# First attention of a hybrid decoder step: token rows on partitions, the norm in a later stage, the combination one step later, the big jobs in the first 24 prompt steps

## The reference, cut to what matters

```
aq, ak = rmsnorm(...), rmsnorm(...)              # 4 heads, two 64-wide maps each
s = einsum('bqhcd,bkhcd->bhcqk', q, k) * scale   # c = 0, 1: the two maps
s = where(dist >= 0, s + bias, -inf)             # causal, ALiBi
p = softmax(s, axis=-1)
a = p[:, :, 0] - lam * p[:, :, 1]
oa = einsum('bhqk,bkhd->bqhd', a, v)
oa = rmsnorm(oa, g_oa) * (1.0 - lam_init)        # over the 128 values of a head
ua = (oa.reshape(B, T, 512) * silu(az)) @ w_branch[0]
```

## Time and profile before

| | us |
|---|---|
| three timed runs, median (lowest to highest) | 1586.78 (1585.46 to 1587.12) |
| the profiled execution, its own time | 1587.19 |
| its span, from the first to the last instruction | 1585.0 |
| PE busy, share of the span | 1507.2, 95% |
| DVE, ACT, POOL busy | 585.4, 397.1, 82.4 |
| mean granted PE clock, share of full | 0.975 |

### The profile page before, as it was taken

How to read it: one execution, slowest core, us unless ns; L and a number is a source line. 1 busy time by engine, 2 the same in 40 slices (tenths; PEclk the granted TensorE clock), 3 DMA queues, 4 the chain that set the end, 5 groups by cost and what they waited for, 6 DMA issues and landing times.

```text
span 1585.0 us, 17452 instructions
## 1 busy us (share of the span) xinstructions
PE 1507.2 (95%) x6810; PEld 1027.9 (65%) x6810; DVE 585.4 (37%) x1321; ACT 397.1 (25%) x874; POOL 82.4 (5%) x109
## 2 busy tenths in 40 slices
PE   6899998999977999999999999999999999999998
PEld 3477665566645544465666665645888778999586
DVE  2444444566565313014545323243333223221321
ACT  2322222444443113102221202123232122121200
POOL 0000001000000000000000000000111101111000
PEclk9899999999997899999999998999999999999999
DMA  9211001010002240000101023100012233210232
GB/s 322 85 60 48 27 30 57 1 54 1 1 0 89 81 149 27 0 20 20 41 21 40 24 60 100 40 1 0 21 49 92 85 109 127 54 47 21 59 100 67
DMA packets 77521, 88.39 MB, mean 56 GB/s; under 512 B 7634, under 2 KB 55394, under 8 KB 77442
## 3 DMA queue, kind: packets, MB, share of 16 engines
q1 hardware_dynamic: 74082, 76.15, 15.7%
q0 software_dynamic: 3360, 11.14, 1.9%
HBM read 76.14 MB, written 11.14 MB: 55 GB/s over the span
## 4 chain that ended last, share of the span: by engine, by line
PE 91%; DVE 3%; ACT 2%; issue 1%; SPq 1%; DMA 1%; POOL 0%; POOLq 0%; DVEq 0%; ACTq 0%
PE heavy L848 32%; PE heavy L794 12%; PE heavy L763 9%; PE heavy L764 9%; PE heavy L765 9%; PE attended L961 2%; PE attended L913 2%; PE scores L893 2%; PE heavy L809 2%; PE scores L936 1%; PE transposed L902 1%; PE scores L1061 1%; PE attended L1233 1%; PE scores L1181 1%; PE scores L1222 1%
## 5 line engine op out<-in xcount | busy, mean ns | idle before, releaser
L848 PE MATMUL heavy<-arena 128*128 128x364 f32 (+3 forms) x1608 | 519.9, 476 | 2.4 <-DMA arena<-w_in 1.8
L848 PEld LDWEIGHTS heavy<-arena 128*128 128x128 f32 (+1 forms) x1608 | 295.6, 189 | 189.0 <-issue 32.1
L794 PE MATMUL heavy<-arena 128*128 128x512 f32 (+1 forms) x496 | 225.0, 610 | 1.9 <-DVE arena L1755 1.9
L1314 ACT ACTIVATE arena<-heavy 128x364 f32<-128x364 f32 (+1 forms) x108 | 51.2, 474 | 489.2 <-PE heavy L848 297.7
L794 PEld LDWEIGHTS heavy<-arena 128*128 128x128 f32 (+1 forms) x496 | 93.0, 191 | 119.1 <-issue 117.7
L763 PE MATMUL heavy<-h_hi,wg_hi 128*128 128x364 f32 (+1 forms) x384 | 129.8, 338 | 0.0
L1725 DVE SCALAR_TENSOR_TENSOR arena<-arena,heavy 128x364 f32<-128x364 f32 (+1 forms) x72 | 38.3, 532 | 240.5 <-PE heavy L848 145.7
L764 PE MATMUL heavy<-h_lo,wg_hi 128*128 128x364 f32 (+1 forms) x384 | 126.4, 329 | 0.0
L765 PE MATMUL heavy<-h_hi,wg_lo 128*128 128x364 f32 (+1 forms) x384 | 126.4, 329 | 0.0
L1708 DVE SCALAR_TENSOR_TENSOR arena<-arena,heavy 128x364 f32<-128x364 f32 (+1 forms) x36 | 19.1, 532 | 157.7 <-ACT arena L1314 157.7
L763 PEld LDWEIGHTS heavy<-h_hi,wg_hi 128*128 128x128 f32 x384 | 72.6, 189 | 2.4 <-issue 1.8
(11 more groups left out here) (246 smaller groups left out, 1930.1 us busy)
## 6 DMA issues: line engine op xcount, KB each, us to landing
arena<-w_in SPq DMA_DIRECT2D x24, 512.0 KB, 4.1
arena<-w_in SPq DMA_DIRECT2D x5, 2048.0 KB, 9.7
arena<-x_prompt SPq DMA_DIRECT2D x16, 512.0 KB, 4.0
arena<-w_in SPq DMA_DIRECT2D x8, 1024.0 KB, 5.8
arena<-w_branch SPq DMA_DIRECT2D x24, 256.0 KB, 4.5
out<-arena POOLq DMA_DIRECT2D x21, 256.0 KB, 2.3
arena<-w_mkv SPq DMA_DIRECT2D x2, 2048.0 KB, 11.8
arena<-cache_k_a SPq DMA_DIRECT2D x16, 256.0 KB, 2.8
```

What stands on the lines that cost most here:

```text
L794: last = nc.tensor.matmul(bank[0:rows, :], src[:, k, r * P:r * P + rows], w[:, k, :], start=(k == 0), stop=(k == KD - 1))
L848: last = nc.tensor.matmul(bank[0:m, 0:cw], w[:, k, :], src[:, k, c0:c0 + cw], start=(k == 0), stop=(k == kb - 1))
L1314: out = nc.scalar.activation(tanh[m % 2][:, 0:cw], bank[:, 0:cw], ACT.Tanh, scale=0.5)
```

## The change

It changes the first attention in five ways.

1. `values` swaps its operands, so that `OB` holds tokens on partitions. ACT copies a finished block out (`attended_evict`) into the place of that block's queries, which are no longer needed, and squares it head by head with the row sum taken along (`attended_square`). The means, roots and reciprocals of all blocks are made at once, on 36 columns, at the start of stage R (`attended_roots`). In stage Z the rows are scaled (DVE `attended_scaled`), transposed (PE `attended_transposed`, four transposes for each of nine tiles), and multiplied into the gate (DVE `attended_gated`). `tail_mean`, `tail_root`, `tail_final` and `tail_copy` remain only for the last tile of the linear attention. The sample rows no longer need a transposition of their own in stage R.
2. `combine(u-1)` stands behind `softmax_head(u)` on DVE; `mx`, `nmx` and the row sums have two places, and the wait for `p_ready` is gone from `softmax_head`.
3. `combine` no longer scales map 0; it adds map 1 times one coefficient, and the reciprocal of map 0's row sum goes into the norm later.
4. The 24 jobs stand in steps 0 to 23, one each; steps 24 to 31 have none.
5. On ACT, `exps(u)` stands ahead of the step's job and of `weights_evict(u-1)`. `page_keys` for the first two sequences waits for the transposes of step 30 instead of its values; the weights `w_gv` of stage V load to another place.

```diff
-MEAN_AT = {u + 1: k for u, k in COPY_AT.items()}
+FIRST_A = 0
 def heavy_A(u):
-    js, n = STAGE["A"], 27
-    return [js[x] for x in range(len(js) * min(u, n) // n, len(js) * min(u + 1, n) // n)]
+    return [STAGE["A"][u - FIRST_A]] if FIRST_A <= u < FIRST_A + 24 else []
...
-        w_gv = at(8704, [KD, W])
+        w_gv = at(13056, [KD, W])
...
+        def attended_rows(r):
+            if r < PT:
+                return qT[:, :, r * P:(r + 1) * P]
+            return og[0:NS_TOK, :].rearrange("p (h d) -> p h d", h=H)
...
                 if b < 2:
-                    sp.wait_ge(pv_done, NU - 1)
+                    sp.wait_ge(tr_full, TRN["a", NU - 2, groups_A(NU - 2)[-1][0]] + 1)
...
-                    last = nc.tensor.matmul(OB[:, h * P:(h + 1) * P], vA[:, b, h * P:(h + 1) * P],
-                                            aT[u % 2][:, b * P:(b + 1) * P], start=(b == 0), stop=(b == i))
+                    last = nc.tensor.matmul(OB[:, h * P:(h + 1) * P], aT[u % 2][:, b * P:(b + 1) * P],
+                                            vA[:, b, h * P:(h + 1) * P], start=(b == 0), stop=(b == i))
...
+            def attended_transposed(r):
+                n = ROWS_TILE(r)
+                pe.wait_ge(ascaled, r + 1)
+                tr_begin("at", r)
+                for h in range(H):
+                    last = nc.tensor.transpose(TR[:, h * n:(h + 1) * n], attended_rows(r)[:, h, :], ident[0:n, 0:n])
+                last.then_inc(tr_full, 1)
...
-                if u in MEAN_AT:
-                    tail_mean(MEAN_AT[u])
-            heavy(STAGE["R"][0])
-            sample_rows_transposed(0)
-            heavy(STAGE["R"][1])
-            tail_mean(PT)
-            heavy(STAGE["R"][2])
+            for n in STAGE["R"]:
+                heavy(n)
...
+            for x, n in enumerate(STAGE["Z"]):
+                heavy(n)
+                if 1 <= x <= PT + 1:
+                    attended_transposed(x - 1)
...
+            def attended_evict(r):
+                n = ROWS_TILE(r)
+                act.wait_ge(pv_done, H * (r + 1) if r < PT else NU + NB)
+                nc.scalar.copy(attended_rows(r), OB[0:n, :].rearrange("p (h d) -> p h d", h=H)).then_inc(o_free, 1)
+            def attended_square(r):
+                n = ROWS_TILE(r)
+                act.wait_ge(o_free, r + 1)
+                if r:
+                    act.wait_ge(asum_ready, r)
+                for h in range(H):
+                    last = nc.scalar.activation(sq[0:n, h * P:(h + 1) * P], attended_rows(r)[:, h, :], ACT.Square,
+                                                accum_out=asum[0:n, H * r + h:H * r + h + 1])
+                last.then_inc(asum_ready, 1)
...
             def softmax_head(u):
-                nk = (i + 1) * P
+                nk, x = (i + 1) * P, 2 * (u % 2)
-                if u:
-                    dve.wait_ge(p_ready, u)
...
             def combine(u):
                 dve.wait_ge(p_ready, u + 1)
-                settle(nc.vector.reciprocal(coef[:, 0:2], psum_r[:, 0:2]))
-                settle(nc.vector.tensor_scalar(coef[:, 1:2], coef[:, 1:2], neg_lam[:, :], None, ALU.mult))
+                settle(nc.vector.reciprocal(arec[:, u, :], psum_r[:, x:x + 2]))
+                settle(nc.vector.scalar_tensor_tensor(out=coef[:, 0:1], in0=arec[:, u, 1:2], scalar=neg_lam[:, :],
+                                                      in1=psum_r[:, x:x + 1], op0=ALU.mult, op1=ALU.mult))
                 p0, p1 = S[u % 2][:, 0, 0:nk], S[u % 2][:, 1, 0:nk]
-                settle(nc.vector.tensor_scalar(p0, p0, coef[:, 0:1], None, ALU.mult))
-                nc.vector.scalar_tensor_tensor(out=p0, in0=p1, scalar=coef[:, 1:2], in1=p0, op0=ALU.mult,
+                nc.vector.scalar_tensor_tensor(out=p0, in0=p1, scalar=coef[:, 0:1], in1=p0, op0=ALU.mult,
                                                op1=ALU.add).then_inc(a_ready, 1)
...
                 if u < NU:
                     softmax_head(u)
+                if 1 <= u <= NU:
+                    combine(u - 1)
```

More of the change, by code:

```diff
@@ L177, in transposed_uses @@
             uses.append(("s", u - 1 - H * PT))
-        if u in MEAN_AT:
-            uses.append(("mean", MEAN_AT[u]))
-    uses.append(("mean", PT))
+    uses += [("at", r) for r in range(PT + 1)]
     for r in range(PT + 1):
         uses.append(("kd", r))
-    uses.append(("mean", PT + 1))
+    uses.append(("mean",))
     uses += [("gt", r) for r in range(PT)]
@@ L338, in hybrid_step @@
         og_rows = at(30720, [H, T])
+        asum, aroot = (at(TAIL + 728 + 512 + (PT + 1) * H * i, [(PT + 1) * H]) for i in range(2))
+        arec = at(TAIL + 728 + 512 + 2 * (PT + 1) * H, [PT * H, 2])
         gsum, groot = (at(TAIL + 728 + 768 + 32 * i, [PT * H]) for i in range(2))
@@ L1836, in tail_copy, with sample_rows_copy @@
                 nc.vector.tensor_copy(og[:, 0:H * n].rearrange("p (k y t) -> p y k t", k=2, y=2),
                                       pair_view(0, n)).then_inc(o_free, 1)
-            def sample_rows_copy(i, done, count):
-                dve.wait_ge(done, count)
-                nc.vector.tensor_copy((otok, otokM)[i][0:NS_TOK, :], OB[0:NS_TOK, :]).then_inc(otok_ready, 1)
-            def tail_final(k, heads):
-                n, z = tail_of(k)
-                g = GOA if k <= PT else GOB
-                h0, h1 = heads
-                roots, out = rs_t[:, h0 * n:h1 * n], og[:, h0 * n:h1 * n]
-                if h0 == 0:
-                    dve.wait_ge(tr_free, TRN["mean", k] + 1)
-                    if k <= PT:
-                        c = min((k * P + n - 1) // CHW, 2)
-                        for x in range(2):
-                            hv_wait_free(dve, STAGE["A"][0] + KW * (c + 1) - 1 - x)
-                    else:
-                        hv_wait_free(dve, STAGE["Z"][-1])
+            def sample_rows_copy():
+                dve.wait_ge(om_full, PT + NB)
+                nc.vector.tensor_copy(otokM[0:NS_TOK, :], OB[0:NS_TOK, :]).then_inc(otok_ready, 1)
@@ L1856, in tail_final @@
+            def tail_final():
+                z = gzT[:, :, NP_TOK:T]
+                roots, out = rs_t[:, 0:H * NS_TOK], og[:, 0:H * NS_TOK]
+                dve.wait_ge(tr_free, TRN["mean",] + 1)
                 settle(nc.vector.reciprocal(roots, roots))
-                settle(nc.vector.scalar_tensor_tensor(out=out, in0=out, scalar=gcol[:, g:g + 1], in1=roots,
+                settle(nc.vector.scalar_tensor_tensor(out=out, in0=out, scalar=gcol[:, GOB:GOB + 1], in1=roots,
                                                       op0=ALU.mult, op1=ALU.mult))
-                ins = nc.vector.tensor_tensor(out=z[:, h0:h1], in0=z[:, h0:h1],
-                                              in1=out.rearrange("p (h t) -> p h t", h=h1 - h0), op=ALU.mult)
@@ L1938, in _ @@
                     heavy(n)
[L1939 to L1949 removed]
+                if NU < u < STEPS_A:
+                    sample_scale(u - NU)
                 if u == NU:
@@ L2057, in _ @@
             nc.vector.memset(St[0], 0.0).then_inc(st_zero, 1)
-            for n in STAGE["Z"]:
+            attended_scaled(0)
+            for x, n in enumerate(STAGE["Z"]):
                 heavy(n)
+                if x <= PT - 1:
+                    attended_scaled(x + 1)
+                if 1 <= x <= PT + 1:
+                    attended_gated(x - 1)
             dve.wait_ge(st_zero, 1)
```

180 lines of the change are left out of this document (81 added, 99 removed).

## The result

The changed kernel takes 1596.28 us, the median of 8 runs (1592.57 to 1600.69). The kernel before, in the same comparison, takes 1586.59 (1585.42 to 1593.03, 8 runs). The ratio is 1.0059 with a 95% interval of 1.0040 to 1.0078: the change makes the kernel slower by 0.6%. The prediction was 1573.9, so it was wrong in sign, by 22 us. The profiled execution took 1594.01 us.

The account below looks back on a forecast made before the run. TensorE, busy 95% of 1585.0 us, was taken as the bound. The sample part's end 15.6 earlier less 2.7 lost in R and Z gave 12.9 off 1587.2: 1574.3, or 1573.9 against the median; range 1563 to 1584.

Parts of the forecast that it names:

- Steps 1 to 23: First attention: three more jobs add 15.3 us; means, idle and slow scores save 5.5, 7.4, 2.1; step 24 starts at 416.3.
- Steps 24 to 31: First attention's jobless steps: serial chain of 62.9 us at full clock plus 6 for low clock, ending at 485.2.
- half of 1.99 for the first map's scores: Steps 24 to 31, 1024 keys: with 0.1 to reach DVE, 1.1 us before the maxima, in a step of 8.45.
- I take the share of before, 22%: Steps 24 to 31: 1.2 GHz for 22%, as in old steps 27 to 31, costing 6 us between 0 and 28.
- some 4.3 of 7.9 us, much like before: Steps 24 to 31: TensorE's predicted busy time per step, the ground for keeping the low-clock share at 22%.
- The key pages: Before the sample part: loads given out at 485.2, pages there at 488.7, 6.5 us more; sample part starts at 495.2, 10.8 earlier.
- The sample part: 78.3 us loses a 2.00 mean and 1.28 table reload; 73.5 taken, 69.6 without clock falls; ends at 568.7, 15.6 gained.
- Stages R and V: After the sample part: R loses transposes (0.39) and the mean (0.63), 1.0 less; no other change named before Z.
- Stage Z: Output stage: nine groups of transposes come in between jobs at 0.43 us a group, 3.7 us more.
- The clock rival: Steps 24 to 31 all at 1.2 GHz (28 instead of 6), pages 8, sample part 75: 1599 us; chance 0.08.
- The cover rival: Half of steps 24 to 31 slow (14), idle stays in steps 1 to 23 (2), later parts 3: 1587, no change; 0.09.
- The full-clock rival: Clock falls nowhere: 0 instead of 6, 5 instead of 6.5, sample part 69.6: 11.4 less, 1562.5 us; chance 0.18.

Follow-up runs that it names:

- e3_fill: Changed kernel with three useless 128x512 matmuls after the scores of each of steps 24 to 31; 1570.83 us, ratio 0.9886 to the kernel before.
- e12_before_fill: Kernel before with three useless matmuls in each of steps 27 to 31 and one in each sample step; 1587.55 us, ratio 1.0002.
- The table of the four kernels: Changed kernel and variants with combination in its own step, jobs over steps 0 to 26, or both; low-clock shares in jobless steps 42%, 30%, 32%, 22%.
- e6_last_fill_sample: Changed kernel with the jobs in steps 8 to 31 and one useless matmul in each of seven sample steps; 1559.28 us, ratio 0.9829.
- e7_last_fill_both: Changed kernel with jobs in steps 8 to 31, one useless matmul per sample step and two in each of steps 1 to 7; 1552.25 us, ratio 0.9779.
- e8_spread_own: Changed kernel with jobs spread over steps 0 to 26 and the combination back in its own step behind the jobs; 1568.76 us, ratio 0.9898.
- e1_jobs_last: Changed kernel with its 24 jobs in steps 8 to 31 instead of 0 to 23; 1566.03 us, ratio 0.9855.
- e5_own_step: Changed kernel with the combination back in its own step, behind the step's job; 1581.32 us, ratio 0.9945.

## Why the prediction was wrong, step by step

**Steps 1 to 23: right.** Forecast for the scores of step 24: 416.3. Measured: 413.46, and no idle time of TensorE from 242.82 on. TensorE's idle time, the means and the slow scores are gone as forecast. The stage also began 0.9 earlier, and was 1.9 shorter than the sum (170.6 against 172.6), which was not traced further.

**Steps 24 to 31: the step that failed.** The prediction had 62.9 us at full clock and 6 for the clock, 68.9 in all; measured 83.16, 14.3 more. The experiments part this into two terms of the sum:
- "half of 1.99 for the first map's scores" was mis-sized. VectorE's first maximum starts when all eight score records have ended, 1.77 + 0.07 after their start with 896 keys, where 1.0 was taken, and 1.98 + 0.07 with 1024, where 1.1 was. Small savings elsewhere give some back: a step of 896 keys takes 8.26 where the sum had 7.6. e3_fill shows the eight steps at a clock of 1.00: 68.86, so the full-clock sum was 6 too low, 0.7 a step.
- "I take the share of before, 22%" was the larger one. The share was 42%, and its price 83.16 - 68.86 = 14.3, not 6. The price of one microsecond at the low clock was about right: 6 us for 22% of 68.9 is 0.40, and 14.3 for 42% of 83.2 is 0.41. The share was wrong. The argument for 22% was that TensorE was busy "some 4.3 of 7.9 us, much like before". That is 54%, and the row it was compared with has 30.45 of 45.49, which is 67% (some 60% with its slow pieces at full speed, an estimate from e12_before_fill). And it was read in five jobless steps with the combination in its own step. The table of the four kernels shows what was left out: the share goes up by about 10 points with the combination behind the maxima, and by about 10 with eight jobless steps in a row instead of five. In the changed kernel TensorE waits once in each step for the combination, 33.6 us in eight, up to 4.6 at a time. That the longer wait raises the share with the one move fits the table, but no run changes the wait alone; why eight such steps have a higher share than five, at the same longest wait, stays open.

That e3_fill lands on the 68.9 of the forecast is chance: 6 too little in the sum at full clock, and 6 for a low clock that this run does not have.

**The key pages: right in kind, 1.5 too long.** The loads were given out at 496.80, behind the end of step 31, as the new wait says. The way to the sample part took 8.5 us (10.0 forecast), and TensorE's pieces in it ran at full clock, which is the case for which the forecast had named 5 instead of 6.5.

**The sample part: its clock was mis-sized too.** Forecast 73.5, measured 81.1. The mean and ScalarE's table load are gone from it, and the value of that was about right: in e3_fill, with a clock of 0.96, the part takes 71.6 us, where the forecast had 69.6 for no fall at all. But the batches alternate between full and low clock. From the chain of the changed kernel, scores and values of successive batches, with other pieces left out at the marks:

```profile
529.71 2.30 PE scores L935 x8
...
534.54 5.27 PE attended L960 x24
539.82 3.99 PE scores L935 x8
...
546.34 3.83 PE attended L960 x24
550.17 2.30 PE scores L935 x8
```

The same 24 value matmuls take 3.83 and 5.27 us, the same eight score matmuls 2.30 and 3.99.

**Stages R and V: not foreseen.** Forecast 1.0 less than the 82.2 us that the kernel before needs from 584.30; measured 84.96 from 586.21, clock 0.95 against 1.00 over 81.7 us of the kernel before. 3.8 us too many. In e3_fill, with a sample part at 0.96, the stretch up to the first transposes of Z is the same (95.0 us, 94.9 in the changed kernel), so this loss does not come from the jobless steps. Where it lies can be read: the work that was to go is gone (stage R is 0.6 shorter), but the clock is low from the last sample batch (values 6.16 us instead of 3.83) until some 1.4 us into stage R, and again from 611.5 to 618.3, in and behind the small scores of stage V, although TensorE is never idle between. At half speed these 8.2 us cost 4.1. The kernel before has a clock of 1.00 in both places. Why it falls there stays open.

**Stage Z: right.** Nine groups of transposes stand between the jobs, at the 0.43 us read from the earlier trace rows. The first, from the chain of the changed kernel:

```profile
681.15 0.44 PE transposed L982 x4
```

The errors add up: -2.8 to step 24, +14.3, -1.5 at the pages, +7.6, +3.8 make 21.4 on the 1574.3 of the forecast, and 1595.7 is 1.7 from the profiled 1594.0. Most of the 1.7 lies behind 671.17, where the changed kernel takes 921.0 us and the kernel before 918.5: 2.5 more, where 3.7 was forecast.

**The rivals.** The clock rival (1599) came nearest to the time, though its mechanism was reached only in part: not all, but 42% of the steps' time was at 1.2 GHz. It named 60% of the steps as the point from which the kernel is slower; with 6 of the forecast's gain of 12.9 used up by the full-clock sum, that point lay at some 44% by its own terms (25 us from 22% to 100%). The cover rival had the clock's price right (14 instead of 6) and the rest of its terms wrong: no idle time stayed in steps 1 to 23, and the sample part took more than the upper end it had. The full-clock rival is refuted by the granted clock of 0.79. The Trainium skill (TensorE: Matmul & The Clock Gate, section "HAM oscillation — how this bites in real kernels") describes bursts with waits between them that find the clock low. The traces agree for the changed kernel's jobless steps (waits of 4.2 us in the mean, clock 0.79). I weighed the rule by what the kernel before had shown in a shorter stretch with another order on VectorE.

## What to carry over

Do not carry the share of low clock over from the code before: here one place on VectorE and three more jobless steps each raised it by about 10 points, from 22% to 42%, while a microsecond at the low clock cost about 0.4 us in both kernels. Where TensorE's pieces lie on the path one after another with waits between them, covering work is worth more than its own time, and so is the order of two instructions on another engine (here up to 15 us). Put covering jobs under the longest steps and leave the shortest uncovered, and put an operation for the step before ahead of, not behind, what waits for the current step. Useless matmuls in the waits of the bound engine are a cheap test for the clock, and gained 25 us, or 1.6%, in the changed kernel; in the kernel before they gained nothing, since where they fell on the path they cost what the clock gave back, and in its sample part they did not hold the clock. So count the time, not the clock.

## What was unexpected of the hardware

- The clock was low with TensorE busy for 92% of the time and waits of 0.4 to 1.3 us: 74.23 of 81.10 us in the sample part, clock 0.84, alternating batch by batch. One more matmul of 0.9 us in each wait brought it to 0.98 in e6_last_fill_sample and 0.96 in e7_last_fill_both, but left it at 0.90 in e12_before_fill.
- The sample part of e3_fill stayed near full clock without any matmul added to it (0.96 against 0.84), and that of e8_spread_own stayed full up to its last two batches. e1_jobs_last also entered it at full clock and fell at 509.8, after three batches. What decides between them is open; whether it is what came before, or chance from run to run, no profile here can tell.
- The time follows the mean clock also between runs of one kernel: the changed one took 1592.57 us at 0.970 and 1600.69 at 0.963; e5_own_step 1570.68 at 0.979 and 1587.56 at 0.966.
